# Retention's values for two heads at once: 512-column products ahead of q and k instead of 256-column products behind them

## The reference, cut to what matters

```
qk      = einsum('bnihd,bnjhd->bnhij', q, k) * decay        # 128 x 128
o_inner = einsum('bnhij,bnjhe->bnihe', qk, v)
kv      = einsum('bnjhd,bnjhe->nbhde', k_dec, v)            # 128 x 256
s_n+1   = chunk_decay * s_n + kv_n                          # scan over the chunks
o_cross = einsum('bnihd,nbhde->bnihe', q_dec, s_prev)
o       = o_inner + o_cross, then normed over its 256 columns
ret     = silu(g) * o
```

## Time and profile before

| | |
|---|---|
| Median of 3 runs (lowest to highest) | 2537.79 us (2537.73 to 2538.15) |
| The profiled execution's own time | 2537.46 us |
| Its span | 2535.6 us |
| PE busy | 2491.5 us, 98% of the span |
| DVE, ACT, POOL busy | 1510.9, 1068.8, 190.6 us |
| Granted TensorE clock, mean | 0.999 |
| Chain that ended last | PE 88%, DVE 7%, ACT 2% |

### The profile page before, as it was taken

The page is one execution under the profiler, slowest core; times in us unless marked ns, Lnnn a source line. Parts: engine busy times, 40 slices in busy tenths (PEclk is TensorE's granted clock), DMA queues, the critical chain, the costliest instruction groups (busy, mean ns, idle before and its releaser), DMA issues.

```text
span 2535.6 us, 30521 instructions
## 1 busy us (share of the span) xinstructions
PE 2491.5 (98%) x11808; PEld 2054.9 (81%) x11808; DVE 1510.9 (60%) x2211; ACT 1068.8 (42%) x1708; POOL 190.6 (8%) x173
## 2 busy tenths in 40 slices
PE   7999999999999999999999999999999999999998
PEld 6777888888888888888888887866788888888886
DVE  4345223223533786877664754358767687776668
ACT  4344322222322564444434542357526544444433
POOL 0000000000020300000000110145111000000000
PEclk9999999999999999999999999999999999999999
DMA  4221211111421566779865541101215577788554
GB/s 167 69 73 67 75 42 36 41 34 51 166 76 59 183 211 219 241 254 334 301 248 183 187 155 65 34 20 41 109 58 208 187 244 258 261 332 321 189 187 170
DMA packets 148304, 390.06 MB, mean 154 GB/s; under 512 B 15136, under 2 KB 15392, under 8 KB 148032
## 3 DMA queue, kind: packets, MB, share of 16 engines
q1 hardware_dynamic: 148160, 388.11, 43.5%
HBM read 284.17 MB, written 100.73 MB: 152 GB/s over the span
## 4 chain that ended last, share of the span: by engine, by line
PE 88%; DVE 7%; ACT 2%; issue 2%; DMA 1%; POOL 0%; SPq 0%; DVEq 0%; ACTq 0%; POOLq 0%
PE bank L660 27%; PE bank L662 27%; PE bank L661 27%; DVE PAl L2402 1%; PE bank L734 1%; DVE st L2397 1%; DVE wlo L1757 1%; PE bank L784 1%; PE bank L851 1%; PE bank L1119 1%; PE bank L861 0%; PE bank L855 0%; PE bank L819 0%; DMA rbx<-wp_d 0%; ACT PAh L1697 0%
## 5 line engine op out<-in xcount | busy, mean ns | idle before, releaser
L1757 DVE TENSOR_TENSOR wlo<-raw,whi 128x1024 fp32r<-128x1024 f32 x122 | 149.4, 1233 | 255.2 <-ACT whi L1192 254.6
L660 PE MATMUL bank<-hhi,whi 128*128 128x512 f32 x608 | 248.7, 409 | 1.7 <-DVE hlo L1782 1.7
L662 PE MATMUL bank<-hhi,wlo 128*128 128x512 f32 x608 | 238.4, 392 | 0.0
L661 PE MATMUL bank<-hlo,whi 128*128 128x512 f32 x608 | 238.2, 392 | 0.0
L1192 ACT ACTIVATE whi<-raw 128x1024 fp32r<-128x1024 f32 x122 | 127.2, 1053 | 115.3 <-PE bank L662 89.8
L1490 ACT ACTIVATE r<-r 128x512 f32<-128x512 f32 x96 | 60.6, 632 | 190.6 <-DVE r L2227 133.2
L660 PEld LDWEIGHTS bank<-hhi,whi 128*128 128x128 f32 x608 | 114.7, 189 | 29.3 <-issue 6.7
L662 PEld LDWEIGHTS bank<-hhi,wlo 128*128 128x128 f32 x608 | 114.5, 188 | 25.2
L661 PEld LDWEIGHTS bank<-hlo,whi 128*128 128x128 f32 x608 | 114.9, 189 | 22.4
L660 PE MATMUL bank<-yhi,whi 128*128 128x512 f32 x192 | 74.9, 390 | 0.0
L662 PE MATMUL bank<-yhi,wlo 128*128 128x512 f32 x192 | 74.7, 389 | 0.0
(11 more groups left out here) (457 smaller groups left out, 7073.3 us busy)
## 6 DMA issues: line engine op xcount, KB each, us to landing
raw<-wp_d SPq DMA_DIRECT2D x122, 512.0 KB, 3.6
ra<-ud_d SPq DMA_DIRECT2D x112, 512.0 KB, 4.5
rawp<-wp_d SPq DMA_DIRECT2D x32, 1024.0 KB, 5.8
ud_d<-us SPq DMA_DIRECT2D x128, 256.0 KB, 5.5
rbh<-wp_d SPq DMA_DIRECT2D x64, 512.0 KB, 5.8
ud_d<-f SPq DMA_DIRECT2D x96, 256.0 KB, 2.2
rbw<-wp_d SPq DMA_DIRECT2D x48, 512.0 KB, 3.5
rbx<-wp_d SPq DMA_DIRECT2D x32, 512.0 KB, 8.2
```

The lines of the kernel that those rows point to most:

```text
L660: e.matmul(P, sh, mh, start=first, stop=False, skip_group_check=more)
L661: e.matmul(P, sh, ml, start=False, stop=False, skip_group_check=more)
L662: return e.matmul(P, sl, mh, start=False, stop=last, skip_group_check=more)
L1757: e.tensor_tensor(out=wlo[n % SLOTS][:, :], in0=raw[n % RAWS][:, :], in1=whi[n % SLOTS][:, :].bitcast(F32), op=ALU.subtract).then_inc(*up( ...
```

## The change

v_r is made for two heads at once, by `token_wide` with 512 weight columns and four pieces: for heads 0 and 1 ahead of q and k of head 0, before the first chain, and for heads 2 and 3 in head 1's chain, ahead of q and k of head 2. `token_major` and its product go. ACT copies each tile's 512 columns with two instructions into two buffers; a third one, `rv2`, holds head 2's values and head 3 takes head 0's. Main has then 16 units for heads 0 and 2 and 24 for head 1 (g 1 to 8, v 9 to 16, q and k 17 to 24), and the ratios are 0.8, 1.2, 0.8 and 1.0. PE waits at a head's first step for k's copy and for v's tile 7. Four buffers of later stages (`lsig`, `swahi`) change places.

```diff
-def token_major(feed, token_product, name, col, spec):
-    ns = [feed.piece("T", name, col, 0), feed.piece("T", name, col, 4)]
...
-def token_wide(feed, wide_product, name, spec):
-    ns = [feed.piece("V", name, k) for k in range(4)]
+def token_wide(feed, wide_product, name, col, spec):
+    ns = [feed.piece("V", name, k, col) for k in range(4)]
     for t in range(NT):
         wide_product(ns, t, spec)
         if t == 7:
             for n in ns:
                 feed.done(n)
         yield
...
     def proj(h):
+        if h % 2 == 0:
+            yield from token_wide(feed, wide_product, "v_r", 256 * h, v(h // 2))
         yield from feature_major(feed, half_product, "q_r", h, q(h))
         yield from feature_major(feed, half_product, "k_r", h, k(h))
-        yield from token_major(feed, token_product, "v_r", 256 * h, v(h))
...
     for h in range(4):
-        interleave(main(h), retention(h), 1.2 if h < 3 else 1.0)
+        interleave(main(h), retention(h), (0.8, 1.2, 0.8, 1.0)[h])
...
+    rv2 = at("rv2", XO + 24, [128, NT, 256])
+
+    def rv_of(h):
+        return (rv[0], rv[1], rv2, rv[0])[h]
...
                 if n == 0:
-                    e.wait_ge(*ok("free", "v_r", h, 7))
+                    e.wait_ge(*ok("free", "k_r", h, 1))
+                    e.wait_ge(*ok("free", "v_r", h // 2, 7))
...
-                e.activation(rv[h % 2][:, t, :], bank_of("v_r", h, t)[:, 0:256], ACT.Copy).then_inc(*free("v_r", h, t))
+                e.activation(rv_of(2 * p)[:, t, :], bank_of("v_r", p, t)[:, 0:256], ACT.Copy)
+                e.activation(rv_of(2 * p + 1)[:, t, :], bank_of("v_r", p, t)[:, 256:512], ACT.Copy).then_inc(*free("v_r", p, t))
```

More of the change, by code:

```diff
@@ L357, in swa_order, with retention_order @@
         yield from values(n)
-def retention_order(feed, half_product, token_product, q, k, v, g, lgate, retention, gates_left):
+def retention_order(feed, half_product, wide_product, q, k, v, g, lgate, retention, gates_left):
     def proj(h):
+        if h % 2 == 0:
+            yield from token_wide(feed, wide_product, "v_r", 256 * h, v(h // 2))
         yield from feature_major(feed, half_product, "q_r", h, q(h))
         yield from feature_major(feed, half_product, "k_r", h, k(h))
-        yield from token_major(feed, token_product, "v_r", 256 * h, v(h))
     def main(h):
@@ L501, in programs @@
     tb = at("tb", FO + 72.5, [128, 128])
-    lsig = [at(f"lsig{i}", FO + o, [128, T]) for i, o in enumerate((0, 8, 16, 20))]
+    lsig = [at(f"lsig{i}", FO + o, [128, T]) for i, o in enumerate((0, 8, 24, 28))]
     rethi = at("rethi", HO, [128, 8, T], F32R)
-    swahi = [at(f"swahi{k}", FO + o, [128, T], F32R) for k, o in enumerate((4, 12, 24, 28))]
+    swahi = [at(f"swahi{k}", FO + o, [128, T], F32R) for k, o in enumerate((4, 12, 16, 20))]
     retlo = at("retlo", XO, [128, 8, T], F32R)
@@ L682, in half_product @@
             yield
[L684 to L695, removed]
         def wide_product(ns, t, spec):
@@ L850, in retention @@
                 e.wait_ge(*ok("ss", h, n))
-                x = e.matmul(P[:, 0:256], ss[n % 2][:, :], rv[i][:, n, :], start=True, stop=n == 0)
+                x = e.matmul(P[:, 0:256], ss[n % 2][:, :], rv_of(h)[:, n, :], start=True, stop=n == 0)
                 if n > 0:
@@ L860, in retention @@
                     e.wait_ge(*ok("free", "rt", h, n))
-                    e.matmul(P[:, 0:256], kd[:, :], rv[i][:, n, :], start=True, stop=True).then_inc(*ring.full("kv", h, n))
+                    e.matmul(P[:, 0:256], kd[:, :], rv_of(h)[:, n, :], start=True, stop=True).then_inc(*ring.full("kv", h, n))
                 yield
@@ L874, in retention @@
                 yield
-        retention_order(feed, half_product, token_product,
+        retention_order(feed, half_product, wide_product,
                         lambda h: (("q_r", h), hhi, hlo, None), lambda h: (("k_r", h), hhi, hlo, None),
-                        lambda h: (("v_r", h), hhi, hlo), lambda h, m: (("g_r", h, m), hhi, hlo, None),
+                        lambda p: (("v_r", p), hhi, hlo), lambda h, m: (("g_r", h, m), hhi, hlo, None),
                         nothing, retention, lambda: gates(range(13, 16)))
@@ L1059, in tensor_program @@
         interleave(qk_products(), idle(14), 1.5)
-        run(token_wide(feed, wide_product, "v_2", (("v_2",), yhi, ylo)))
+        run(token_wide(feed, wide_product, "v_2", 0, (("v_2",), yhi, ylo)))
         tally.alias(("v2_end",), ring.latest)
@@ L1336, in scalar_program, with values_evac @@
         interleave(gates(range(13), sig, ("ht", 7)), swa_order(swa_scores, swa_values), 0.95)
-        def values_evac(h):
+        def values_evac(p):
             def evac(t):
-                e.wait_ge(*ok("full", "v_r", h, t))
-                if t == 0 and h > 1:
-                    e.wait_ge(*ok("full", "ro", h - 2, 7))
-                e.activation(rv[h % 2][:, t, :], bank_of("v_r", h, t)[:, 0:256], ACT.Copy).then_inc(*free("v_r", h, t))
+                e.wait_ge(*ok("full", "v_r", p, t))
+                if t == 0 and p:
+                    e.wait_ge(*ok("full", "ro", 0, 7))
+                    e.wait_ge(*ok("free", "O", 7, 1))
+                e.activation(rv_of(2 * p)[:, t, :], bank_of("v_r", p, t)[:, 0:256], ACT.Copy)
+                e.activation(rv_of(2 * p + 1)[:, t, :], bank_of("v_r", p, t)[:, 256:512], ACT.Copy).then_inc(*free("v_r", p, t))
             return evac
@@ L1670, in scalar_program @@
         e.activation(QM[0][1][64:128, :], q2[64:128, 0, :], ACT.Copy).then_inc(*up("qx", 0))
-        run(token_wide(feed, token_product, "v_2", v2_evac))
+        run(token_wide(feed, token_product, "v_2", 0, v2_evac))
         def pooled(g):
@@ L2383, in vector_program @@
             e.memset(QM[0][j][o + 32:o + 34, :].bitcast(F32), 1.0).then_inc(*up("aux", 0, j, 2))
-        run(token_wide(feed, token_product, "v_2", v2_low))
+        run(token_wide(feed, token_product, "v_2", 0, v2_low))
         def pooled(g):
@@ L2965, in sync_program @@
         feed.cap = CAT
-        run(token_wide(feed, nothing, "v_2", None))
+        run(token_wide(feed, nothing, "v_2", 0, None))
         def duplicates(t):
@@ L3082, in pack @@
             wp[n].reshape(128, 8, 128)[:] = w[:, 128 * d[2]:128 * d[2] + 128].reshape(8, 128, 128).transpose(1, 0, 2)
-        elif d[0] == "T":
-            wp[n].reshape(128, 4, 256)[:] = w[128 * d[3]:128 * d[3] + 512, d[2]:d[2] + 256].reshape(4, 128, 256).transpose(1, 0, 2)
         elif d[0] == "V":
-            wp[n].reshape(128, 2, 512)[:] = w[256 * d[2]:256 * d[2] + 256].reshape(2, 128, 512).transpose(1, 0, 2)
+            wp[n].reshape(128, 2, 512)[:] = w[256 * d[2]:256 * d[2] + 256, d[3]:d[3] + 512].reshape(2, 128, 512).transpose(1, 0, 2)
         elif d[0] == "B":
```

## The result

| | before | with the change |
|---|---|---|
| Median of 15 runs each | 2538.61 us | 2543.36 us |
| Lowest to highest | 2536.38 to 2541.04 | 2540.86 to 2544.68 |
| Ratio, 95% interval | | 1.0019 (1.0012 to 1.0026) |
| Profiled execution: own time, span | 2537.46, 2535.6 us | 2544.68, 2542.9 us |

The change costs 4.8 us of the median. The forecast was 5.5 us, and the line of 0.2% ran through its range. The interval leaves out 1.0000, so the change is slower beyond the noise, and it takes in 1.0020.

A forecast was written before the change was run, and what follows sets the result against it. The prediction took PE's stream to bound the kernel. Its terms, -5.1 + 2.6 + 6.3 + 1.7 = +5.5 us on 2537.46, gave 2543.0 us (0.22% slower), with a range from 2535.5 to 2546.5 us.

The forecast's parts named there:

- Bound by PE's stream: Whole kernel: PE is busy 98% of the span, so a saving or new wait in its stream counts in full.
- Part 1: Value products: 384 matmuls of 512 columns replace 768 of 256, by distance of starts saving 5.1 us.
- The issue formula: Value products: the skill's columns / 2.4 + 2.5 ns per matmul would make the saving only 1.0 us; chance 0.02.
- Part 3: Retention chain, heads 0 and 2: rt and ro issued together at four places wait for `ss`, 0.65 us each, +2.6 us.
- the old wait: PE's wait for `ss` behind a g piece, once each in heads 0, 1 and 2; moves in 0 and 2, sum zero.
- Part 4: Head 1's chain after v's tile 7: four pieces given back at once delay chunk 6's `ss`, PE waits 6.3 us.
- Part 5: Behind the new hole in head 1: products restart at the 1.2 GHz level, losing 1.7 us, bounds 0 and 3.4.
- the clock stays: Rival: the clock keeps its upper level in head 1's hole, giving 2541.3 us, within 0.2%; chance 0.17.
- Part 6: Norm after ro(7) in heads 0 and 2: slack suffices, so 0, at most 0.5 us a head.

The follow-up runs named there:

- the narrow form: The change with chain steps of heads 0, 1 and 2 moved by tables, its value products taken back to 256 columns: 2537.16 us, ratio 0.9996 against before.
- The run with one piece a unit: The change, with the four weight pieces of heads 2 and 3's values given back one per unit instead of all at once: 2536.17 us, ratio 0.9990 against before.
- those with two and three: The change, with two or three of the four weight pieces given back at once in head 1, the rest later: 2536.86 us with two, 2536.85 with three.
- the moved chain: The change, four pieces still given back at once, head 1's chain steps moved so none follows within three units: 2534.62 us, ratio 0.9984 against before.
- the pair edit: The change, with a table of steps in heads 0 and 2 that never puts rt(n) beside ro(n): 2541.03 us, ratio 1.0008 against before.
- the later ro(6): The change, four pieces still given back at once, with head 1's ro(6) moved from unit 17 to unit 18: 2540.59 us in one execution.

## Why the prediction was right, point by point

- **Bound by PE's stream.** Right: the chain stays PE's for 89%, and every us of the stage is one of PE's stream.
- **Part 1, products, -5.1 us.** Right: 5.44 us a tile, and 4.7 us come back when the narrow form is put in the same place. That is 0.4 short of 5.1; of it 0.25 lies behind head 1's values, where the two programs do not differ. The issue formula's 1.0 us, weighed there, does not hold here: at 256 columns the rows show 0.120 us a product, not 0.109.
- **Part 3, adjacent steps, +2.6 us.** Right: four waits, 0.63 us each. That the old wait leaves unit 5 and comes back at unit 9 in heads 0 and 2 held too: heads 0 and 2 have one wait of 0.46 us each between the new ones (at 385.2 and 556.6 us), and head 1 keeps its own.
- **Part 4, the burst, +6.3 us.** Right: 6.1 us, with the high parts, the transfer and `ss` within 0.3 us of the times written down. The run with one piece a unit, those with two and three, and the moved chain each took away what this working says.
- **Part 5, the clock, +1.7 us.** The mechanism was right, the size off: 2.9 us in the profiled execution, within the bounds and nearer to the upper one of 3.4. The term that was mis-sized came from the start of the program, as the nearest row. At the start of the program (as the change's trace has it) the granted clock reads 0.50 already in the stretch 18 to 22 us, ahead of its dense products at 21.7, so part of the slow stretch likely lay on idle time. Behind the hole the clock fell some 0.7 us before PE restarted (the stretch 496 to 497 us still reads 0.98), and nearly the whole slow stretch lay on work. The rival "the clock stays" is out in all three profiles with a hole of 3.4 us or more (the change, the pair edit and the later ro(6)).
- **Part 6, the norm, 0.** Right: PE waits for nothing at L856.
- **The sum.** +5.5 forecast, +6.6 in the profiled stage, +4.8 between medians. The mechanism held; that the total came so near is in part luck. With the clock sized as the trace has it the same sum would have been +6.7, 1.9 over the medians, and the low clock term offset this. The profiled execution of the change lies 1.3 us over its median and that of before 1.2 under its own, so the profile overstates the median's difference. In the other versions that were timed, stage and medians tell the difference from before within 0.9 us of each other; here they lie 1.8 apart. How long the clock stays low differs between the profiles of two kernels with nearly the same hole, but whether this is the reason stays open: the kernel before has no such hole and spreads by 4.7 us all the same.

The measured ratio of 1.0019 falls just inside the 0.2%, to which 0.45 had been given, against 0.48 for slower: by a hair not the outcome that was held likeliest, though the direction is the one forecast and clear of the noise.

## What to carry to other kernels

When two small work items are merged into one of double size, look at what is released at its end: here twice as many buffers came free at once, and an in-order engine refilled all of them before a short operation that the bottleneck was waiting for. Release them one by one, or keep the waiting step away from the burst. Either turned the loss of 0.2% into a gain of 0.1 to 0.2%. And write down how long the hole in TensorE's stream is: here one of 2.6 us cost only itself, and one of 3.4 us was paid a second time by the clock.

## What the runs showed of the hardware that was not expected

- A hole of 2.6 us between dense products left the granted clock at 1.00; one of 3.4 us and those of about 6 us lowered it to 0.50, for 3.5 to 6.1 us of the work behind it, at a cost of 1.6 to 2.9 us. "TensorE: Matmul & The Clock Gate" of the Trainium skill (Part 1, HAM oscillation) says that a long enough gap has to be paid by a throttled start. The traces agree for the holes of about 6 us, which restart at the low level. In the run with the hole of 3.4 us the start itself was still fast, and the clock fell only about 0.5 us after PE had resumed.
- The granted-clock column can miss a slow stretch: at the beginning of the program the products of before start 0.43 us apart, and still its stretch from 22 to 24 us reads 1.00, where that of the change, with the same spacing, reads 0.50. The distance of starts is the surer sign. Before:

```profile
22.00:24.00 2.00, 2.00 (x6) 1.00 0.28 113
```

With the change:

```profile
22.00:24.00 2.00, 2.00 (x5) 0.50 0.28 113
```
